# One 512-column matmul on [high|low] activations in 63 weight tiles, and 512 columns of weights in the value tiles

## The reference

```
h = rmsnorm(x, norm_mix_g);  proj = h @ w_in           # bg cg xv q k v z a b ga gb
y_a = (bg * conv3(cg * xv)) @ w_a_out
y_b = gated_delta_rule(silu(conv4(q,k,v)), ..., a, b) normed * silu(z) @ w_b_out
x = x + (sigmoid(ga) * y_a + sigmoid(gb) * y_b) @ w_o
x = x + conv_ffn(rmsnorm(x), w_up, w_down)
# second block
qa, ka, va, qr, kr, vr, gr, gate_a, gate_b = split(xn @ w_in_2)
o_a = dilated attention(rmsnorm(qa), rmsnorm(ka), va)
o_r = head_groupnorm(retention(qr, kr, vr)) * silu(gr)
x = x + (sigmoid(gate_a) * (o_a @ w_proj_a) + sigmoid(gate_b) * (o_r @ w_proj_b)) @ w_out
x = x + square(relu(rmsnorm(x) @ w_up_2)) @ w_down_2
```

## Time and profile before

| | |
|---|---|
| three runs | 1221.56, 1225.92, 1215.78 us; median 1221.56 |
| the profiled execution | 1218.03 us, of it 1216.1 us span; granted TensorE clock 0.99 |
| TensorE busy | 1165.5 us, 9690 matmuls |
| DVE busy | 781.0 us (64%) |
| ACT busy | 609.1 us (50%) |
| POOL busy | 305.6 us (25%) |
| DMA | 192.91 MB, mean 159 GB/s |

### The profile page before, as it was taken

One profiled execution on the slowest core, in us unless ns is written; L12 is line 12 of the kernel. 1 busy time (PEld: TensorE's weight loads), 2 busy tenths in 40 slices (PEclk: granted clock), 3 DMA queues, 4 the chain that ended last, 5 costly groups with the idle time before them and its releaser, 6 DMA issues.

```text
span 1216.1 us, 22170 instructions
## 1 busy us (share of the span) xinstructions
PE 1165.5 (96%) x9690; PEld 1138.5 (94%) x9690; DVE 781.0 (64%) x847; ACT 609.1 (50%) x700; POOL 305.6 (25%) x175
## 2 busy tenths in 40 slices
PE   5988999999999899999989999999999999999998
PEld 5887999999999899999979999999998999899998
DVE  5997785555355577677658966755565655765453
ACT  4877432243274465455456643442498544543431
POOL 3343364421023134234235520000011010421010
PEclk9988999999999999999999999999999999999999
DMA  6433331123245444554545454333543555455552
GB/s 245 168 119 139 118 139 71 70 70 139 105 155 196 170 173 167 183 193 157 203 139 186 174 190 174 140 134 144 182 155 114 208 193 189 145 213 197 200 184 102
DMA packets 27744, 192.91 MB, mean 159 GB/s; under 512 B 3072, under 2 KB 3072, under 8 KB 4992
## 3 DMA queue, kind: packets, MB, share of 16 engines
q1 hardware_dynamic: 27648, 191.49, 43.7%
HBM read 190.43 MB, written 1.05 MB: 157 GB/s over the span
## 4 chain that ended last, share of the span: by engine, by line
PE 59%; issue 13%; ACT 10%; DVE 8%; POOL 8%; DMA 2%; POOLq 0%; SPq 0%; ACTq 0%; DVEq 0%
PE psS L527 32%; PE psA L527 9%; PE psS L515 6%; POOL t L1548 6%; ACT wh L847 4%; DVE wl L1164 3%; DVE acc L1167 2%; DMA raw<-in_wts 2%; PE psA L659 1%; PE psA L673 1%; DVE Xl L1167 1%; PE psA L677 1%; ACT L831 1%; POOL ss L1548 1%; DVE gdn L1164 1%
## 5 line engine op out<-in xcount | busy, mean ns | idle before, releaser
L1164 DVE TENSOR_TENSOR wl<-raw,wh 128x2048 fp32r<-128x2048 f32 (+1 forms) x174 | 403.8, 2321 | 207.6 <-ACT wh L847 207.0
L847 ACT ACTIVATE wh<-raw 128x2048 fp32r<-128x2048 f32 x176 | 336.5, 1913 | 295.2 <-PE psS L527 145.2
L527 PE MATMUL psS<-Yh,wh 128*128 128x256 f32 x1056 | 304.5, 288 | 13.4 <-DVE Yl L1167 7.9
L527 PE MATMUL psS<-Yl,wh 128*128 128x256 f32 x1056 | 295.9, 280 | 0.0
L527 PE MATMUL psS<-Yh,wl 128*128 128x256 f32 x1056 | 295.8, 280 | 0.0
L527 PE MATMUL psS<-Xh,wh 128*128 128x256 f32 x896 | 265.0, 296 | 20.3 <-DVE wl L1164 13.5
L527 PE MATMUL psS<-Xh,wl 128*128 128x256 f32 x896 | 252.1, 281 | 0.0
L527 PE MATMUL psS<-Xl,wh 128*128 128x256 f32 x896 | 252.1, 281 | 0.0
L527 PEld LDWEIGHTS psS<-Yh,wh 128*128 128x128 f32 x1056 | 200.9, 190 | 19.4 <-issue 9.4
L527 PEld LDWEIGHTS psS<-Yl,wh 128*128 128x128 f32 x1056 | 200.0, 189 | 2.6 <-issue 1.9
L527 PEld LDWEIGHTS psS<-Yh,wl 128*128 128x128 f32 x1056 | 199.7, 189 | 0.0
(11 more groups left out here) (239 smaller groups left out, 2144.1 us busy)
## 6 DMA issues: line engine op xcount, KB each, us to landing
raw<-in_wts SPq DMA_DIRECT2D x176, 1024.0 KB, 4.8
xT<-in_x SPq DMA_DIRECT2D x2, 512.0 KB, 6.3
raw<-in_wts SPq DMA_DIRECT2D x2, 512.0 KB, 7.3
gdn<-in_x SPq DMA_DIRECT2D x1, 1024.0 KB, 6.8
out<-xT SPq DMA_DIRECT2D x4, 256.0 KB, 2.2
xT<-in_sel SPq DMA_DIRECT2D x1, 512.0 KB, 6.3
xf<-in_dr SPq DMA_DIRECT2D x1, 512.0 KB, 5.8
xT<-in_mask SPq DMA_DIRECT2D x1, 384.0 KB, 5.5
```

The costliest lines, as they stand in the source:

```text
L527: mm = pe.matmul(bank[:, half], a[:, n % 3, p, :], b[:, kk_, :], start=(first and i == 0), stop=(last and i == 2), skip_group_check=True)
L847: act.activation(wh[:, n % 3], raw[:, n % 2], ACT.Copy).then_inc(sem["wh"], 1)
L1164: dve.tensor_tensor(out, a, b, op).then_inc(sem[name], 1)
```

## The change

In 63 tiles (gb1 to gb3, z, wb, qa, ka, gr, ta, tb, pb, u2; the list `WIDE`) the high and the low part of the activations now lie in one tensor (X, Y, Z), and one matmul takes wh on [high|low], 512 moving columns, into a bank of its own: the first half holds wh on high, the second wh on low. The product of wl and high is added to the first half. So a tile is 32 matmuls instead of 48, and a result lies in two banks, in four pieces. At the eviction ACT first copies the second halves to SBUF (`minor`), DVE adds the first halves to that, and then scales.

The PSUM tensors psS have two banks each, and psA 4 and 5 are the second banks of these. Where psA 4 and 5 were used beside wide tiles, other banks are used: psA 0 for the norms, psA 2 and 3 for the retention.

The value tiles take their blocks in another order: a pair of tiles holds 4 x 128 columns, the first tile rows 0 to 3 and the second rows 4 to 7. `values` streams 512 columns of weights against 128 positions: 24 matmuls of 512 columns for a tile instead of 48 of 256. Results of a pair are two banks, the first complete in the middle of the second tile (semaphore vt), the other at its end; the first tile of a pair has no eviction, the second has two. In the first tile's second half TensorE needs the bank of the tile just before.

```diff
+    if kind in ("va", "vr"):
+        return "w_in_2", [(k, COL2[kind] + c) for k in range(4 * (j % 2), 4 * (j % 2) + 4)
+                          for c in range(4 * (j // 2), 4 * (j // 2) + 4)]
...
+WIDE = [key for key in SEQ if key[0] in ("z", "wb", "qa", "ka", "gr", "ta", "tb", "pb", "u2")
+        or key in (("gb", 1), ("gb", 2), ("gb", 3))]
+SUMS = {key: i + 1 for i, key in enumerate([key for key in WIDE if key in RING])}
...
-        psS = [ctx.enter_context(nc.psum_tensor(f"psS{i}", [P, 2, S], F32)) for i in range(2)]
-        psA = [ctx.enter_context(nc.psum_tensor(f"psA{i}", [P, 2, S], F32)) for i in range(6)]
+        psS = [ctx.enter_context(nc.psum_tensor(f"psS{i}", [P, 2, 2, S], F32)) for i in range(2)]
+        psA = [ctx.enter_context(nc.psum_tensor(f"psA{i}", [P, 2, S], F32)) for i in range(4)]
+        psA += [psS[0][:, 1], psS[1][:, 1]]
...
# TensorE, in stream(n)
+                    if key in WIDE:
+                        bank = wide(key)[:, c % 2]
+                        both = {id(Xh): X, id(Yh): Y, id(Zh): Z}[id(h)][:, :, kk_]
+                        pe.matmul(bank, wh[:, n % 3, p, :], both, start=(fresh and p < 2), stop=False,
+                                  skip_group_check=True)
+                        mm = pe.matmul(bank[:, 0], wl[:, n % 3, p, :], h[:, kk_, :], start=False, stop=(p >= 14),
+                                       skip_group_check=True)
                         continue
...
+            def values(n, i):
+                kind, j = SEQ[n]
+                t, k = i // 4, 4 * (j % 2) + i % 4
+                key = (kind, j - j % 2 + t)
+                if j % 2 == 0 and i % 4 == 0:
+                    pe.wait_ge(sem["ev"], GRP[key] - 1)
...
+                for q, (a, b) in enumerate(((Yh, w[0]), (Yl, w[0]), (Yh, w[1]))):
+                    mm = pe.matmul(o, a[:, k, t * P:(t + 1) * P], b, start=(k == 0 and q == 0),
+                                   stop=(k == 7 and q == 2), skip_group_check=True)
+                if j % 2 and i == 3:
+                    mm.then_inc(sem["vt"], 1)
...
# ACT
+            def minor(n):
+                key = kind, j = SEQ[n]
+                if key not in SUMS:
+                    return
+                act.wait_ge(sem["mm"], n + 1)
...
+                act.activation(dst, wide(key)[:, :, 1], ACT.Copy).then_inc(sem["sm"], 1)
...
+                minor(n)
                 if n + 3 < NB and n not in URGENT:
                     split(n + 3)
...
# DVE, in take(n)
+                def whole(dst):
+                    dve.wait_ge(sem["sm"], SUMS[key])
+                    tt(dst, wide(key)[:, :, 0], dst, ALU.add, "sd")
+                    dve.wait_ge(sem["sd"], SUMS[key])
+
+                def scaled(dst, factor):
+                    if key in SUMS:
+                        whole(dst)
+                        tt(dst, dst, factor, ALU.mult, "ev")
+                    else:
+                        tt(dst, ps, factor, ALU.mult, "ev")
...
-                    stt(y[j % 2][:], ps, 0.0, two(rb[:]), ALU.max, ALU.mult, "ev")
+                    whole(y[j % 2][:])
+                    stt(y[j % 2][:], y[j % 2][:], 0.0, two(rb[:]), ALU.max, ALU.mult, "ev")
```

More of the change, by code:

```diff
@@ L379, in ring, with wide @@
         def ring(key):
+            return psS[GRP[key] % 2][:, 0]
+        def wide(key):
             return psS[GRP[key] % 2]
@@ L484, in stream @@
                 fresh = True
-                if key in RING or kind == "pb":
+                if (key in RING and kind not in ("va", "vr")) or kind == "pb":
                     fresh = not (kind == "pb" and j % 2)
@@ L538, in norm @@
                     for half in range(2):
-                        mm = pe.matmul(psA[5][:, g], ones, ss[g][:, half], start=(half == 0), stop=(half == 1),
+                        mm = pe.matmul(psA[0][:, g], ones, ss[g][:, half], start=(half == 0), stop=(half == 1),
                                        skip_group_check=True)
@@ L1184, in take @@
                 key = kind, j = SEQ[n]
-                if key not in RING:
+                if key not in RING or (kind in ("va", "vr") and j % 2 == 0):
                     return
-                dve.wait_ge(sem["mm"], n + 1)
-                ps = ring(key)[:]
+                if kind in ("va", "vr"):
+                    dve.wait_ge(sem["vt"], j // 2 + 1 + (3 if kind == "vr" else 0))
+                else:
+                    dve.wait_ge(sem["mm"], n + 1)
+                ps = ring(key)
+                def whole(dst):
[6 more added lines that the diff above has]
+                        tt(dst, dst, factor, ALU.mult, "ev")
+                    else:
+                        tt(dst, ps, factor, ALU.mult, "ev")
                 if kind in YKINDS:
@@ L1218, in take @@
                         dve.wait_ge(sem["rb"], 3)
-                    tt(pair({"qa": qa, "ka": ka, "qr": qr, "kr": kr}[kind], j), ps, two(rb[:]), ALU.mult, "ev")
+                    scaled(pair({"qa": qa, "ka": ka, "qr": qr, "kr": kr}[kind], j), two(rb[:]))
                 elif kind in ("va", "vr"):
-                    if kind == "va" and j == 0:
+                    if kind == "va" and j == 1:
                         dve.wait_ge(sem["rtk"], 1)
-                    if kind == "vr" and j == 0:
+                    if kind == "vr" and j == 1:
                         dve.wait_ge(sem["as"], 8)
-                    tt((va if kind == "va" else vr)[:, :, j * S:(j + 1) * S], ps,
-                       rtok[:].unsqueeze(2).broadcast_to([P, 2, S]), ALU.mult, "ev")
+                    for t in range(2):
+                        if t:
+                            dve.wait_ge(sem["mm"], n + 1)
+                        dst = (va if kind == "va" else vr)[:, t, (j - 1) * S:(j + 1) * S]
+                        dve.tensor_scalar(dst, ring((kind, j - 1 + t)).rearrange("p a b -> p (a b)"), rtok[:, t:t + 1],
+                                          None, ALU.mult).then_inc(sem["ev"], 1)
                 elif kind == "pb":
```

60 lines of the change are left out of this document (46 added, 14 removed).

## The result

| | median (range, runs) | profiled execution |
|---|---|---|
| before | 1218.67 us (1215.59 to 1225.92, 4) | 1218.03 us |
| changed | 1244.17 us (1243.30 to 1245.16, 4) | 1245.16 us |

The changed kernel is slower: ratio 1.0201, 95% interval 1.0149 to 1.0253. The forecast was 1239, the range 1222 to 1250. Between the two profiled executions lie 27.1 us, where the prediction's sum had 21.2.

What follows compares the result with a forecast made beforehand. TensorE, busy 1165.5 of 1216.1 us, was taken as the bound, late behind ACT or DVE in three stages. Terms 7.7 + 8.0 + 5.0 + 0.5 = 21.2 us on 1218.03 gave 1239 us, range 1222 to 1250.

Steps and rivals of the forecast that it cites:

- The matmul side: Wide and value tiles: time goes with columns, not instructions, so merging saves 0 us, within bounds of 0 to 14.8.
- A: z to wo: ACT's copies and DVE's second passes lengthen the loops and delay the start of wo2; +7.7 us.
- B: qa to va0: DVE's added pass makes it the bound, 6.3 us a turn; +8.0 us, low end 1, high end 10.
- the eight passes: DVE's run of passes at 678.47 in ka, 4.29 us long, counted in full and expected to be stretched.
- C: gr4 to tb2: ACT's turns grow by 0.66 us each, so acc and ta3's eviction come later; +5.0 us.
- Start of u2: At the start of u2 the first two evictions are already late, so the added passes cost 0.5 us.
- The tail: After the last interruption 31 tiles run at one pace, quick or slow, a difference of 6.6 us.
- rival 3: Worse than the sum: POOL holds up the new pass in B and z, or 31-tile tail slow; 1246 to 1250, chance 0.13.
- Rival 1: The added passes are mostly hidden in A, B, C and u2's start; 1227 us, chance 0.24.
- Rival 2: Faster, in all merged pairs: the cost is per instruction, saving 9 to 15 us; 1203 to 1209 at best, chance 0.07.
- What the new profile should show: 512-column steps of 0.227 to 0.236 us, ACT's splits 6.6 (z) and 8.2 (gr) apart, wb0 stall over 3, wo2 7 to 8 later.

Runs made afterwards that it cites:

- e2: The changed kernel without ACT's copy and the addition: one DVE pass on the first halves, leaving out high weights times low activations; 1228.27 us, ratio 1.0079.
- e4: The kernel before with only the value tiles changed, no wide tile; 1217.03 us, ratio 0.9990.
- e6: The kernel before with only qa and ka wide (12 tiles), old value tiles; 1221.33 us, ratio 1.0024.
- e3: The kernel before with only the 24 tiles of pb and u2 wide, old value tiles; 1227.53 us, ratio 1.0077.
- e12: e2 with each 512-column matmul in pb and u2 issued as two of 256; 1221.63 us, ratio 1.0020.
- e8: The kernel before with a single wide tile, u2 8, and old value tiles; 1220.59 us, ratio 1.0022.
- e11: The changed kernel with each 512-column matmul in pb and u2 alone issued as two of 256; 1243.66 us, ratio 1.0193.
- e1: The changed kernel with each 512-column matmul of the wide tiles issued as two of 256, evictions as changed; 1235.97 us, ratio 1.0141.

## Why the prediction was right, and where it was not

**The matmul side, 0:** right, for the instructions. 512 columns step at 0.24 us in the slow and 0.23 in the quick stream or the value tiles; e2 and e4 show no gain. What I left out is that the merged form chooses the pace.

**A, 7.7:** 6.15. The mechanism held: splits later, wb0's t late, a turn longer by 0.73 (I said 0.8). Too large was the copy, 0.48 us to the next instruction where I took 0.66 from the nearest row, a pass with a bias and another function; with it gb3's split came 3.3 us late, counted from gb1, and not 4.1. And one step was wrong: wb0's copy does not stand behind the table load and the sigmoid, but ahead of them:

```profile
381.34 0.60 ACT L909 ACTIVATE t<-psS 128x512 f32<-128x512 f32 x1 [0.20 <-PE psS L531]
381.95 1.28 ACT L982 ACT_TABLE_LOAD   x1
```

So the backlog at wb0's t was 4 us and not 5.3.

**B, 8.0:** 5.1, or 5.8 counted from qa0. DVE was the bound as said, and its scalings kept their 2.70 us beside POOL; that assumption held. A turn is 6.15 and not 6.3, nine of them 1.35; and the eight passes took 3.25 us instead of the 4.29 of the earlier trace rows, where I feared that they would stretch. The reason is POOL. Before, its pass at 678.30 lay beside the first of the eight, which took 1.52 us, the other seven 0.47 each; in the changed kernel all eight take 0.47, in a pause of POOL of 4.86 us. e2 has it as before, e6 as the changed kernel:

```profile
678.30 1.42 POOL L1548 TENSOR_TENSOR Zl<-sq,Zh 128x512 fp32r<-128x512 f32 x1 [3.44 <-issue]
...
695.51 3.02 POOL L1634 TENSOR_TENSOR sq<-mix 128x512 f32<-128x512 f32 x1 [4.86 <-DVE mix L1227]
```

(The first row is from before.) The added pass took 0.69 us every time, but it says nothing on whether it would stretch beside POOL: POOL's square waits for this very pass, and in qa and ka no work of POOL ever lay beside it. The value tiles' earlier need, measured apart, is 0.9.

**C, 5.0:** 4.3, by the same 0.48 for the copy: acc came 6 x 0.49 = 2.9 late instead of 4.0. TensorE began tb1 4.8 us late, where I had 5.8, and got 0.5 of it back before tb2, where I had 0.7.

**Start of u2, 0.5:** nothing in itself. In the norm of u2 0 TensorE stood 2.02 us from start to start in one gap before, and 1.48 in the changed kernel; the slower tiles ahead had taken up the rest. But the small stall that it leaves at u2 3 can turn the pace.

**The tail:** the step that failed. I wrote that a stretch keeps its pace until something interrupts it and gave the slow tail a chance in rival 3, as if the change had no hand in it, for 31 tiles. It came out at 9.4 us, over 47 tiles, in the changed kernel, e2 and e3, the traces with merged matmuls in pb and u2. The 6.1 us behind u2 0 are due to these (e2 against e12, e8). For the 3.3 up to u2 0 that is not shown, as four of nine kernels without merged ta and tb are slow there too. The trace of before has matmuls of 512 columns beside the slow pace and beside the quick one, but nowhere the two sizes in alternation, so no row showed this. Terms A, B and C had been put 4.5 to 5 us too high together and the tail 8.9 too low (9.4 against the 0.5 for the start of u2); 2.2 us lie in no term. So 1239 against 1244 is in part a cancellation: luck.

**Rivals.** Rival 1 (mostly hidden) fell in A and C and, with 5.1, in B. Rival 2 fell by the steps of 0.23 and 0.24 and by e4. Rival 3 happened in its second half; its first did not, since POOL was idle beside the new pass in z and in ka. What the new profile should show came true for the steps, for DVE in ka and for the longer turns of ACT in z and gr, these 6.43 and 8.00 instead of 6.6 and 8.2; wo2 was 6.2 late, not 7 to 8; wb0's stall of over 3 us did not come in one piece, since the z tiles before it had already lost part of it.

**Open:** what sets the pace after a stall, and why the alternation of 512 and 256 columns brings the slow one. That the two are one cause is not shown, nor that it is the alternation: the value tiles, with 512 columns alone, also have weights and activations exchanged, and no run has merged matmuls without those of 256 columns between them. The best of all versions is e4, and that is the same as the kernel before.

## What to carry to other kernels

Merging two matmuls that share a weight block saves what the instruction cost beyond its columns. Where the trace shows none, there is nothing to save, and a second PSUM bank to empty is paid in full on the engines that evict. Price it by those engines' loops, where a queue in order has no slack. And compare the pace of unchanged instructions behind a change: 4% on a long tail cost 6 to 9 us here, as much as the dearest of the waits or more.

## What the runs showed of the hardware

- TensorE has two paces for the same fp32r matmul at a granted clock of 1.00: 113.4 and 117.8 ns for 256 columns. The alternation of 512 and 256 columns was always slow, in e8 from its second pair on, and handed the pace to ordinary matmuls behind it (e8). Value tiles of 512 columns alone took 0.229 us each, between the two; the ordinary tiles behind them were quick in e4 (kr0, gr0) but slow in e2 and e11 (kr0).
- In tb0 of the changed kernel TensorE waited 1.83 us, and then the granted clock fell to the lower of its two levels for some 3 us. The stretch by time, and its matmuls:

```profile
949.00:954.00 5.00, 4.83 (x21) 3.88 (x20) 4.25 (x5) 3.09 (x8) 0.00 (x0) 0.66 0.40 118
```

```profile
948.59 0.47 PE L529 MATMUL psS<-Y,wh 128*128 128x512 f32 x1 [1.83 <-issue]
...
949.81 0.63 PE L529 MATMUL psS<-Y,wh 128*128 128x512 f32 x1
950.45 0.63 PE L529 MATMUL psS<-Y,wh 128*128 128x512 f32 x1
...
953.34 0.66 PE L844 MATMUL psA<-par,acc 128*128 128x128 f32 x4 [0.17 <-DVE acc L1574]
```

  A pair takes 0.64 us (949.81 to 950.45) instead of 0.35. It cost almost nothing: the transposes need acc, which came 0.17 us after TensorE was ready; before, that wait was 1.33 us. In e1 TensorE waited 1.88 us at the same place, the clock stayed at 1.00, and tb0 took 9.85 us as against 9.86: there the wait for acc was 1.77 us. Here a lower clock in front of a wait was paid out of the wait, and a wait of this length was not followed by it every time.
- A pass of ACT that only copies 128x512 from PSUM holds the next instruction up by 0.48 us, though its own row shows 0.58.
